# Attention steps of a two-layer hybrid decoder, written out two at a time

## The reference

```
z = rms_norm(x) @ w_in            # 1024 x 5640: q, k, v, gate_a, forget, u, vb, gate_b, g_a, g_b
q, k = rms_norm per head;  logf = log_sigmoid(forget)
s = q k^T / 8 + (c_q - c_k), causal, c = cumsum(logf);  attn = softmax(s) @ v      # 8 heads of 64
b = u * spatial(vb) * silu(gate_b);  a = attn * silu(gate_a)
m = sigmoid(g_a) * (a @ w_pa) + sigmoid(g_b) * (b @ w_pb);   x = x + m @ w_out
```

## Time and profile before

| | |
|---|---|
| median of 3 runs | 2068.89 us |
| profiled execution | 2073.18 us, its span 2071.4 us |
| PE busy | 1940.2 us (94% of the span), 11188 matmuls and transposes |
| DVE, ACT, POOL busy | 971.5, 673.4, 510.9 us |
| chain that ended last | PE 76%, DVE 9%, issue 7% |
| DMA queue q1 | 176.41 MB, 29.5% of 16 engines |

### The profile page before, as it was taken

How to read it: one execution, slowest core, us unless ns; L and a number is a source line. 1 busy time by engine, 2 the same in 40 slices (tenths; PEclk the granted TensorE clock), 3 DMA queues, 4 the chain that set the end, 5 groups by cost and what they waited for, 6 DMA issues and landing times.

```text
span 2071.4 us, 30982 instructions
## 1 busy us (share of the span) xinstructions
PE 1940.2 (94%) x11188; PEld 1780.4 (86%) x11188; DVE 971.5 (47%) x2302; ACT 673.4 (33%) x1487; POOL 510.9 (25%) x519
## 2 busy tenths in 40 slices
PE   5999899999997999999988999999998989999998
PEld 5889898999877889997778998989997778999986
DVE  4546465554164335454434555656533633444531
ACT  4334344344232222113223344444432332221110
POOL 3513233332012113111134233333311121131110
PEclk9999999999998999999999999999999989999999
DMA  5231313122214323524314113131321243226141
GB/s 152 69 87 48 84 50 94 49 75 79 66 42 136 89 64 85 182 79 146 110 52 104 52 49 93 40 97 48 91 68 52 63 137 92 68 79 206 54 163 51
DMA packets 217804, 178.39 MB, mean 86 GB/s; under 512 B 50261, under 2 KB 191077, under 8 KB 217653
## 3 DMA queue, kind: packets, MB, share of 16 engines
q1 hardware_dynamic: 217652, 176.41, 29.5%
HBM read 131.65 MB, written 44.71 MB: 85 GB/s over the span
## 4 chain that ended last, share of the span: by engine, by line
PE 76%; DVE 9%; issue 7%; ACT 3%; DMA 2%; POOL 2%; SPq 0%; POOLq 0%; DVEq 0%; ACTq 0%
PE bank L75 21%; PE bank L77 20%; PE bank L76 20%; PE bank L1285 2%; PE bank L1298 2%; DVE sg_sT L1472 2%; PE bank L2050 1%; PE bank L1299 1%; PE bank L1268 1%; PE bank L1270 1%; PE bank L2073 1%; DVE at_prob L1165 1%; DVE at_ptlo L1181 1%; PE bank L1245 1%; PE bank L2038 1%
## 5 line engine op out<-in xcount | busy, mean ns | idle before, releaser
L75 PE MATMUL bank<-keep_hhi,at_fhi 128*128 128x384 f32 (+1 forms) x768 | 264.0, 344 | 14.7 <-ACT at_th L933 14.7
L76 PE MATMUL bank<-keep_hlo,at_fhi 128*128 128x384 f32 (+1 forms) x768 | 256.5, 334 | 0.0
L77 PE MATMUL bank<-keep_hhi,at_flo 128*128 128x384 f32 (+1 forms) x768 | 256.4, 334 | 0.0
L75 PE MATMUL bank<-aw_whi,keep_hhi 128*128 128x384 f32 (+3 forms) x576 | 199.2, 346 | 7.1 <-POOL aw_wlo L436 5.2
L75 PE MATMUL bank<-keep_hhi,bw_whi 128*128 128x384 f32 (+1 forms) x576 | 196.7, 341 | 2.2 <-POOLq L2282 2.2
L76 PE MATMUL bank<-aw_wlo,keep_hhi 128*128 128x384 f32 (+3 forms) x576 | 196.7, 341 | 0.0
L77 PE MATMUL bank<-aw_whi,keep_hlo 128*128 128x384 f32 (+3 forms) x576 | 196.5, 341 | 0.0
L979 ACT ACTIVATE at_prob<-at_prob,at_nmx 128x128 f32<-128x128 f32 (+7 forms) x128 | 99.5, 777 | 280.2 <-DVE at_nmx L1172 280.1
L76 PE MATMUL bank<-keep_hlo,bw_whi 128*128 128x384 f32 (+1 forms) x576 | 189.6, 329 | 0.0
L77 PE MATMUL bank<-keep_hhi,bw_wlo 128*128 128x384 f32 (+1 forms) x576 | 189.5, 329 | 0.0
L1181 DVE TENSOR_TENSOR at_ptlo<-bank,at_pthi 128x512 fp32r<-128x512 f32 x192 | 106.2, 553 | 157.8 <-ACT at_pthi L989 157.8
(11 more groups left out here) (252 smaller groups left out, 4413.2 us busy)
## 6 DMA issues: line engine op xcount, KB each, us to landing
at_stage<-in_w_in SPq DMA_DIRECT2D x160, 128.0 KB, 2.6
mg_gate<-gates SPq DMA_DIRECT2D x32, 544.0 KB, 5.3
gates<-at_th SPq DMA_DIRECT2D x64, 192.0 KB, 2.3
br_stage<-in_w_in SPq DMA_DIRECT2D x40, 256.0 KB, 3.3
at_stage<-in_w_in SPq DMA_DIRECT2D x48, 192.0 KB, 2.5
at_decay<-ncum SPq DMA_DIRECT2D x16, 512.0 KB, 4.1
br_k<-in_cache_k SPq DMA_DIRECT2D x32, 256.0 KB, 3.0
br_v<-in_cache_v SPq DMA_DIRECT2D x32, 256.0 KB, 3.0
```

Source lines behind the costliest of these rows:

```text
L75: nc.tensor.matmul(out, sh, mh, start=start and i == 0, stop=False)
L76: nc.tensor.matmul(out, sh, ml, start=False, stop=False)
L77: last = nc.tensor.matmul(out, sl, mh, start=False, stop=stop and i == n - 1)
```

## The change

The loop over the 96 steps takes two at a time. Where before the list ran T n, V n-2, what is due at n, filler, and then the same for n+1, it now runs T n, T n+1, the tanh steps that are open, V n-2, V n-1, what is due at n and n+1, and twice the filler. The `X` steps that are due are held back (`turned`) and put ahead of the next pair's transposes, so behind the filler. No instruction is added or removed.

```diff
-    for n in range(len(steps) + LAG):
-        if n < len(steps):
-            plan.append(("T",) + steps[n])
+    turned = []
+    for n in range(0, len(steps) + LAG, 2):
+        due = after.pop(n, []) + after.pop(n + 1, [])
+        plan += turned
+        turned = [s for s in due if s[0] == "X"]
+        plan += [("T",) + s for s in steps[n:n + 2]]
         fill.read(0)
-        if n >= LAG:
-            plan.append(("V",) + steps[n - LAG])
-            h, G, j = steps[n - LAG]
+        for h, G, j in steps[max(0, n - LAG):n - LAG + 2]:
+            plan.append(("V", h, G, j))
             if j == 4 * G + 3:
                 plan.append(("O", h, G))
-        for s in after.pop(n, []):
+        for s in due:
+            if s[0] == "X":
+                continue
             if s[0] == "Z":
                 fill.before_z()
                 spent += 2
             plan.append(s)
-        while spent + fill.at - first < total * (n + 1) / (len(steps) + 1) and fill.at < len(fill.pieces):
+        while spent + fill.at - first < total * (n + 2) / (len(steps) + 1) and fill.at < len(fill.pieces):
             fill.half()
```

## The result

| | before | after |
|---|---|---|
| median of 5 runs each, alternating on one chip | 2069.84 us (2067.11 to 2073.10) | 2078.71 us (2076.40 to 2080.82) |
| ratio, 95% interval | | 1.0043 (1.0028 to 1.0058) |
| profiled execution | 2073.18 us | 2076.40 us, its span 2074.7 us |

The order by pairs is slower, by 8.9 us or 0.43%: little, but the interval leaves out no change. The forecast was 2070.2 us, no measurable change; the measured time lies in the range of 2057 to 2081.

What follows compares the result with a forecast made beforehand. PE, busy 94% of the span, was taken as the bound, so only its waits count. Terms summed to 1.3 us slower, put on the 2068.89 us median: 2070.2 us, eight-in-ten range 2057 to 2081.

Steps and rivals of the forecast that it cites:

- 1, merged steps save PE work: Attention phases: half of the 192 runs of T steps vanish, 0.4 us of PE time gained, bounds 0 and 2.9.
- 2, waits for the sum: First V of a group: all 14 waits for the output sum go, 11.3 us gained without the two in head 2.
- 3, rows 4 and 5 together: Score row 5 directly behind row 4 waits for DVE's maximum, 0.7 to 2.4 us outside head 2: 13.2 us lost.
- 3, head 0: Head 0: its three score waits for DVE's maximum grow by 0.15 us, 0.3 us lost in all.
- 4, head 2, waits: Head 2: tanh wait 5.8 us in layer 0, 3.3 in layer 1, other waits shrink: 1.3 us gained in all.
- 5, two tanh at once: Heads 6 and 7: filler waits for tanh steps queued behind two copies on ACT, 4.4 us lost, bounds 0 and 7.
- 6, the phase's end: Each attention phase's end: less time from PE's last matmul to the gate's store, 3.6 us gained, bounds 1 and 5.
- the clock: Behind the wait in head 2: the same low granted clock as before, no difference, bounds 4 us each way.
- The slower rival by the weights: Head 2: second filler weight late in both layers, 2077.5 us; 0.24 together with rows 4/5 and tanh losses at upper bounds.
- the fall at the four long waits: Rival: clock falls at four long waits of each layer, 8 falls costing 16 us, 2086 us; chance 0.07.
- The granted clock leaves 0.98: Sign: the forecast is wrong if the granted clock of the two attention phases leaves 0.98.
- the faster one: Rival: score waits cheaper, no tanh waits, shorter low clock in head 2; 11.5 us gained, 2057.4 us; chance 0.27.

Runs made afterwards that it cites:

- the four profiles: One first and one second profile each of the kernel before (2073.18 and 2066.47 us) and the changed kernel (2076.40 and 2077.98 us).
- Row 5 apart: Score row 5 of heads 1 to 7 behind the pair's filler, in the changed kernel: 2057.97 us; behind next projection or filler half, kernel before: 2081.45 us.
- the second profile: The kernel before, unchanged, profiled once more in one execution: 2066.47 us.

## Why the prediction was right, and where it was not

The time is in the range and 8.5 us above the forecast. It is outside the forecast's own band of 2065 to 2075; no change had 0.42, and what came, slower, had 0.31. The range held because its upper end left room for a few falls of the clock, which is what happened. Step by step, in us per execution, positive for gained, the waits with the same margins that the prediction added:

| step | forecast | found |
|---|---|---|
| 1, merged steps save PE work | 0.4 | 2.1, left over |
| 2, waits for the sum | 11.3 | 11.3, all 14 gone |
| 3, rows 4 and 5 together | -13.2 | -14.0 |
| 3, head 0 | -0.3 | about 0 |
| 4, head 2, waits | 1.3 | 2.9 |
| 5, two tanh at once | -4.4 | -4.3 |
| 6, the phase's end | 3.6 | 2.8 |
| the clock | 0 | -9.4 |

The sum of the first seven is 0.8, where -1.3 was forecast; with the clock it is -8.6. The loops of the four profiles make it -10.2, so 1.6 us of small waits has no row in this table. That the sum comes so near to the measured 8.9 is partly luck, since the clock's term is from two executions of each.

**Part 3** hit place by place: 1.91 + 0.17 against 2.1 in heads 1 and 3, 2.29 + 0.17 against 2.4 in head 4, 1.68 against 1.8 less 0.17 in head 6, 0.92 and 0.91 in heads 2 and 5, 0.74 in head 7. The price was read from DVE's queue ahead of one wait and one more low part, and that was enough. Row 5 apart took these waits away, and the time followed.

**Part 4** had the size right in layer 1 (3.3 forecast, 3.59 found) and not in layer 0 (5.8 forecast, 3.29 found). Its own terms give 0.5 more in both: 25.2 us, less 17.9 of PE work and 1.0 of waits ahead, leave 6.3, and 3.8 in layer 1; the latter is what was found, with the margin. The forecast took the late landing of the second filler weight, 2.30 us of ACT's idle time, for a property of layer 0. It was one of the order before: there it was 1.48 us in the second profile and 0.42 us in layer 1, and in after it is 0.55 [the row at 238.70] and 0.67. From T(1,1,4) to PE's release it is now 22.5 us in layer 0 (218.18 to 240.63), where the forecast had 25.2, and 22.7 in layer 1, where it was 22.8 before; why the landing itself is sooner I can't tell from the rows of SP, which issues both loads in the same spacing. The slower rival by the weights is refuted with it.

**The step that failed is the clock**, in two places of part 4 and of the rivals. The prediction put it at "no difference" in head 2 (1.7 us less was found, within chance) and gave the fall at the four long waits 0.07. It happened at nine of sixteen of them: 4.5 falls an execution at 1.7 us is 7.7 us, the term that the sum lacks; head 0 makes up the rest. The rival itself had 8 falls at 2 us. The evidence cited against it, six waits of 1.3 to 1.6 us with no fall behind them (1.17 to 1.43 as the trace writes them), was true, and was evidence about waits of that length. The new ones are 1.7 to 2.3 as the trace writes them, a length of which the profile of before had no example, and its two waits of 3 us, the tanh in layer 0 and the sum in layer 1, did have one behind them. With no fall at the short ones and a fall at 3 us, a fairer price for eight new waits at about 2 was half of the rival's eight falls at 2 us, 8 us, and not none. The 0.59 of layer 1 was read there as a level; it is the mean of a stretch in which a fall to 0.50 that began at 1270.2 and lasted 3.4 us comes to its end. The other rule weighed there, that transposes do not count as matmuls do (the Trainium skill, "TensorE: Matmul & The Clock Gate", on PE-mode transpose), isn't needed: with the transposes left as they were and the waits gone (row 5 apart), these falls went.

**The sign I named for it was too coarse.** "The granted clock leaves 0.98" could hardly have shown 9.4 us in two phases of 490, which is one hundredth; both kernels read 0.98. The stretches behind the waits show it. The other signs came as named; PE's busy time fell by 2.9 us, close to the 3 that would have spoken against part 1, but it moves by 5 to 10 us between two profiles of one kernel. A slip in the rivals changes nothing: the sum of the faster one leaves out the 0.3 of head 0.

## What to carry to other kernels

When a reordering trades many short waits for fewer long ones, price the length of each and not only the sum: here 102 waits below 1.65 us cost no more than themselves, and half of those at about 2 us cost 1.7 us on top. Before giving up such an order, look at which two steps now touch: two score rows that share a bank and a tanh behind a late weight hid a gain of 34 us, and each took a few lines to part. Some 7 of the 34 lie ahead of the first T and come to single steps as well. A mend belongs to its order: row 5 apart gains 20 us by pairs and loses 12 by single steps.

## What the runs showed of the hardware

**Falls of the clock against the length of the wait.** From all twelve profiles I listed each wait of PE over 0.6 us in heads 1 to 7 (X's left out), and whether the granted clock fell to 0.50 during it or within 1.7 us behind its end:

| idle before the matmul | waits | falls |
|---|---|---|
| 0.6 to 1.62 us | 102 | 0 |
| 1.68 to 2.30 us | 41 | 21 |
| 2.58 to 5.01 us | 19 | 19 |

Two more, of 0.9 us, came while the clock was already low. The middle row is not ordered by length alone: row 5 of head 1 (1.91 us) fell 2 times in 10, of head 3 (1.92) 6, of head 4 (2.29) 4, of head 6 (1.68) 8. In the same kernel the same wait falls in one layer and not in the other, as at 278.18 and 1302.40 above, so a fall of this kind is a matter of chance for one execution and of count for the median. The low stretches in the loops lasted 3.4 us, some 6.8 and two 10.2. In head 0 the order by pairs has waits of 1.50, 0.70 and 0.87 us within 4 us of each other (the last is shorter where the clock has fallen by then). The clock fell there in 10 of 16 layers, though each of these waits alone is in the first class.

The Trainium skill, "TensorE: Matmul & The Clock Gate", section "A second HAM failure mode: psum-queue depth-cycling", says that frequent short idle times between groups of matmuls can make the clock swing between its two levels. This case agrees for waits from 1.68 us on, and for shorter ones where three stand close together as in head 0; single waits up to 1.62 us brought no fall. What decides in the middle class stays open: a run that varied only the work around one wait wasn't made.

**Transposes in longer runs** cost about the same each: seven take 0.69 us from their start to the V behind them (218.18 to 218.87 in after), 0.10 us each, where four took 0.35, 0.09 each.
